# Block inverse of a gated delta step: N used as it stands, forms (U N) transposed at each level

## What is computed

```python
kb = k * beta[..., None]
a_mat = jnp.where(strict, jnp.einsum('bhnid,bhnjd->bhnij', kb, k) * decay, 0.0)
t_mat = lax.linalg.triangular_solve(a_mat + eye, jnp.broadcast_to(eye, a_mat.shape),
                                    left_side=True, lower=True)
u = t_mat @ (v * beta[..., None])
w = t_mat @ (kb * jnp.exp(gc)[..., None])
```

## Time and profile before

| | before |
|---|---|
| median of 3 runs | 2878.22 us |
| profiled execution, first to last instruction | 2873.6 us |
| PE busy | 2854.6 us (99%) |
| DVE busy | 1795.8 us (62%) |
| ACT busy | 1417.1 us (49%) |
| GpSimd busy | 150.7 us (5%) |
| mean DMA rate | 181 GB/s |

### The profile page before, as it was taken

How to read it: one execution, slowest core, us unless ns; L and a number is a source line. 1 busy time by engine, 2 the same in 40 slices (tenths; PEclk the granted TensorE clock), 3 DMA queues, 4 the chain that set the end, 5 groups by cost and what they waited for, 6 DMA issues and landing times.

```text
span 2873.6 us, 68820 instructions
## 1 busy us (share of the span) xinstructions
PE 2854.6 (99%) x25511; PEld 2781.0 (97%) x25511; DVE 1795.8 (62%) x2900; ACT 1417.1 (49%) x2141; POOL 150.7 (5%) x285
## 2 busy tenths in 40 slices
PE   8999999999999999999999999999999999999999
PEld 7999999999999999999999999999999999999999
DVE  7888788888886455555555444587555555554444
ACT  6666566565664444444444343566444444444343
POOL 1112112111110000000000000000000000000000
PEclk9999999999999999999999999999999999999999
DMA  7666656666556555555555555744555555555554
GB/s 226 189 178 188 191 166 194 181 177 188 160 182 198 187 188 178 181 180 178 182 179 180 183 180 181 221 151 130 171 182 179 179 182 178 180 182 179 182 180 152
DMA packets 521091, 518.97 MB, mean 181 GB/s; under 512 B 32128, under 2 KB 444201, under 8 KB 520665
## 3 DMA queue, kind: packets, MB, share of 16 engines
q1 hardware_dynamic: 519150, 510.34, 57.6%
q0 software_dynamic: 1152, 5.58, 0.6%
q10 hardware_dynamic: 594, 0.25, 0.0%
HBM read 492.12 MB, written 32.82 MB: 183 GB/s over the span
## 4 chain that ended last, share of the span: by engine, by line
PE 67%; issue 1%; ACT 0%; DMA 0%; DVE 0%; DVEq 0%; ACTq 0%; POOLq 0%
PE bank L498 11%; PE bank L503 11%; PE bank L499 11%; PE upper L503 11%; PE upper L498 11%; PE upper L499 11%; PE upper L1027 0%; PE upper L1052 0%; DMA x_res<-x_spill 0%; PE upper L1038 0%; PE upper L1089 0%; PE upper L1028 0%; PE upper L1055 0%; ACT scores L812 0%; PE upper L1042 0%
## 5 line engine op out<-in xcount | busy, mean ns | idle before, releaser
L477 DVE TENSOR_TENSOR w_lo<-w_raw,w_hi 128x1024 fp32r<-128x1024 f32 x858 | 1051.2, 1225 | 919.9 <-ACT w_hi L470 917.0
L470 ACT ACTIVATE w_hi<-w_raw 128x1024 fp32r<-128x1024 f32 x858 | 910.1, 1061 | 1241.6 <-PE bank L503 709.1
L498 PE MATMUL bank<-h_hi,w_hi 128*128 128x264 f32 x3168 | 829.6, 295 | 0.4 <-DVE h_lo L585 0.3
L499 PE MATMUL bank<-h_lo,w_hi 128*128 128x264 f32 x3168 | 794.8, 284 | 0.0
L498 PEld LDWEIGHTS bank<-h_hi,w_hi 128*128 128x128 f32 x3168 | 597.3, 189 | 21.3 <-issue 8.8
L499 PEld LDWEIGHTS bank<-h_lo,w_hi 128*128 128x128 f32 x3168 | 598.2, 189 | 1.3
L503 PE MATMUL bank<-h_hi,w_lo 128*128 128x264 f32 x3168 | 449.8, 284 | 0.0
L503 PEld LDWEIGHTS bank<-h_hi,w_lo 128*128 128x128 f32 x3168 | 412.1, 188 | 0.0
L498 PE MATMUL upper<-h_hi,w_hi 128*128 128x264 f32 x1456 | 361.7, 285 | 0.0
L499 PE MATMUL upper<-h_lo,w_hi 128*128 128x264 f32 x1456 | 361.4, 284 | 0.0
L498 PEld LDWEIGHTS upper<-h_hi,w_hi 128*128 128x128 f32 x1456 | 274.3, 188 | 0.0
(11 more groups left out here) (447 smaller groups left out, 3655.5 us busy)
## 6 DMA issues: line engine op xcount, KB each, us to landing
w_raw<-in_w_gate_up_dram SPq DMA_DIRECT2D x704, 256.0 KB, 2.9
w_raw<-in_w_in_a_dram SPq DMA_DIRECT2D x388, 256.0 KB, 3.2
w_raw<-in_w_down_dram SPq DMA_DIRECT2D x352, 256.0 KB, 2.9
w_raw<-in_w_out_a_dram SPq DMA_DIRECT2D x128, 256.0 KB, 3.1
s_dec<-in_state_delta_dram SPq DMA_DIRECT2D x32, 512.0 KB, 6.1
out_dram<-s_dec SPq DMA_DIRECT2D x32, 512.0 KB, 4.9
w_raw<-in_w_q_b_dram SPq DMA_DIRECT2D x64, 256.0 KB, 3.1
w_raw<-in_w_o_b_dram SPq DMA_DIRECT2D x64, 256.0 KB, 2.9
```

The source lines that it names most:

```text
L470: nc.scalar.activation(w_hi[:, s % SPL, :], w_raw[:, s, :], ACT.Copy).then_inc(hi_ready, 1)
L477: ops.tensor_tensor(w_lo[:, s % SPL, :], w_raw[:, s, :], w_hi[:, s % SPL, :].bitcast(F32), ALU.subtract).then_inc(lo_ready, 1)
L498: nc.tensor.matmul(bank[bk][:, 0:T], high(t), xh, start=first, stop=False)
L499: nc.tensor.matmul(bank[bk][:, 0:T], high(t), xl, start=False, stop=False)
```

## The change

The products are formed the other way round. At each level the kernel now computes the transpose of (U N) with `NT` as it stands as stationary operand and the transposed known inverse `Tm` as moving operand. The result `Xm` is then the stationary operand of the second product, and the known inverse, untransposed, the moving one. So no `Nm` is needed: the four TensorE transposes and their copy go. Since in the second product two of the four matrices lie crosswise, ACT makes crosswise copies `Us` of half of `Um` in step 7, and in step 13 a copy of part of `UF` to `Um`. The mask of the 16-wide level is transposed. Because `UF` is the memory of `NT`, and `NT` is now read in step 11, ACT's two copies of the diagonal blocks into `UF` wait for that matmul and stand in step 12. DVE's transpose of the new quarter of `UF` moves from step 13 to step 12, as one instruction, and PE's step 13 waits for it and for ACT's copies. The counts of `inv_pe` fall from 13 to 12 in a group. The diff, cut to this:

```diff
-    halves = [row == col, up & same(16), level(16), level(32)]
+    halves = [row == col, up & same(16), level(16).T, level(32)]
-                Nm = st_("Nm", [P, 4, P])
+                Us = st_("Us", [P, 2, HP])
# ACT
                 elif n == 7:
                     nc.scalar.activation(twos(Um), pair23, ACT.Copy).then_inc(inv_act, 1)
-                    act.wait_ge(inv_pe, 13 * G + 7)
-                    nc.scalar.activation(Nm[:, :, :], B[0][:, :], ACT.Copy).then_inc(inv_act, 1)
-                elif n == 11:
-
-                    act.wait_ge(inv_dve, 15 * G + 10)
+                    for b in range(2):
+                        at, to = slice(HP * b, HP * (b + 1)), slice(HP * (1 - b), HP * (2 - b))
+                        m = nc.scalar.activation(Us[to, :, :], pair23[at, 1, :].rearrange("p (m n) -> p m n", m=2), ACT.Copy)
+                    m.then_inc(inv_act, 1)
+                elif n == 12:
+
+                    act.wait_ge(inv_pe, 12 * G + 9)
                     for b in range(2):
                         at = slice(HP * b, HP * (b + 1))
                         m = nc.scalar.activation(UF[at, :, at], Um[at, :, :], ACT.Copy)
                     m.then_inc(inv_act, 1)
-                elif n == 12:
-                    act.wait_ge(inv_pe, 13 * G + 11)
-                    nc.scalar.activation(Tm[HP:P, 2:4, :], Tm[0:HP, 2:4, :], ACT.Copy).then_inc(inv_act, 1)
                 elif n == 13:
+                    act.wait_ge(inv_dve, 15 * G + 13)
+                    nc.scalar.activation(Um[0:HP, 0:2, :], UF[HP:P, 0:2, HP:P], ACT.Copy).then_inc(inv_act, 1)
# PE
                     each4(pair23, half(Pb), half(Um)).then_inc(inv_pe, 1)
-                    for m_ in range(4):
-                        m = nc.tensor.transpose(B[0][:, m_ * P:(m_ + 1) * P], NT[:, m_, :], ident)
-                    m.then_inc(inv_pe, 1)
                 elif n == 8:
 
+                    inv(inv_dve, 8)
                     inv(inv_act, 6)
-                    each4(pair23, full(Nm), half(Um)).then_inc(inv_pe, 1)
+                    each4(pair23, full(NT), half(Tm)).then_inc(inv_pe, 1)
                 elif n == 10:
                     inv(inv_dve, 9)
-                    each4(pair01, half(Tm), half(Xm)).then_inc(inv_pe, 1)
+                    each4(pair01, half(Xm), lambda m_, b: (Um[block(b), m_, :] if m_ < 2 else Us[block(b), m_ - 2, :])
+                          ).then_inc(inv_pe, 1)
                 elif n == 11:
 
-                    inv(inv_dve, 10)
+                    inv(inv_dve, 11)
...
-                            m = nc.tensor.matmul(B[0][up, m_ * QP:(m_ + 1) * QP], Nm[lo, m_, up],
-                                                 Um[lo, m_, QP:2 * QP], start=True, stop=True)
+                            m = nc.tensor.matmul(B[0][lo, m_ * QP:(m_ + 1) * QP], NT[up, m_, lo],
+                                                 Tm[up, m_, 0:QP], start=True, stop=True)
...
-                            m = nc.tensor.matmul(B[1][up, m_ * QP:(m_ + 1) * QP], Tm[up, m_, 0:QP], Xm[up, m_, 0:QP],
-                                                 start=True, stop=True)
+                            lo, up = quarter(b, 1), quarter(b, 0)
+                            m = nc.tensor.matmul(B[1][up, m_ * QP:(m_ + 1) * QP], Xm[lo, m_, 0:QP],
+                                                 Um[lo, m_, QP:2 * QP], start=True, stop=True)
...
                     inv(inv_act, 7)
-                    inv(inv_dve, 13)
+                    inv(inv_dve, 14)
...
-                            m = nc.tensor.matmul(B[3][block(b), i * HP:(i + 1) * HP], Nm[block(1), m_, block(0)],
-                                                 UF[block(1), m_, block(1)], start=True, stop=True)
+                            m = nc.tensor.matmul(B[3][block(b), i * HP:(i + 1) * HP], NT[block(0), m_, block(1)],
+                                                 Tm[block(0), m_, :], start=True, stop=True)
...
-                            m = nc.tensor.matmul(B[0][block(b), i * HP:(i + 1) * HP], Tm[block(b), 2 * b + i, :],
-                                                 Xm[block(b), i, :], start=True, stop=True)
+                            known = UF[block(1), 2 + i, block(1)] if b else Um[block(0), i, :]
+                            m = nc.tensor.matmul(B[0][block(b), i * HP:(i + 1) * HP], Xm[block(b), i, :], known,
+                                                 start=True, stop=True)
# DVE
                     elif n == 7:
                         dve.wait_ge(inv_act, 9 * G + 5)
-                        nc.vector.transpose(Tm[:, 0:2, :], Um[:, 0:2, :])
-                        for b in range(2):
-                            at, to = slice(HP * b, HP * (b + 1)), slice(HP * (1 - b), HP * (2 - b))
-                            m = nc.vector.transpose(Tm[to, 2:4, :], Um[at, 2:4, :])
-                        m.then_inc(inv_dve, 1)
+                        turned(Tm, Um)
...
                     elif n == 11:
+                        got(9)
+                        nc.vector.tensor_copy(Xm[:, :, 0:QP], m4(B[0][:, 0:P])).then_inc(inv_dve, 1)
+                    elif n == 12:
                         got(10)
-                        nc.vector.tensor_copy(Xm[0:96, :, 0:QP], m4(B[0][0:96, 0:P])).then_inc(inv_dve, 1)
-                    elif n == 12:
-                        got(11)
                         dve.wait_ge(inv_act, 9 * G + 7)
                         for b in range(2):
                             at = HP * b
                             m = ts(UF[at:at + QP, :, at + QP:at + HP], m4(B[1][at:at + QP, 0:P]), -1.0, None, ALU.mult)
                         m.then_inc(inv_dve, 1)
+                        own(13)
+                        nc.vector.transpose(Tm[QP:HP, :, 0:QP], UF[0:QP, :, QP:HP]).then_inc(inv_dve, 1)
                     elif n == 13:
-                        own(13)
-                        dve.wait_ge(inv_act, 9 * G + 8)
-                        for b in range(2):
-                            at = HP * b + QP
-                            m = nc.vector.transpose(Tm[at:at + QP, 2 * b:2 * b + 2, 0:QP],
-                                                    UF[0:QP, 2 * b:2 * b + 2, QP:HP])
-                        m.then_inc(inv_dve, 1)
-                        got(12)
+                        got(11)
                         nc.vector.tensor_copy(Xm[:, 0:2, :], B[3][:, 0:P].rearrange("p (m n) -> p m n", m=2)
                                               ).then_inc(inv_dve, 1)
```

More of the change, by code:

```diff
@@ L1694, in step @@
                 elif n == 4:
-                    act.wait_ge(inv_pe, 13 * G + 1)
+                    act.wait_ge(inv_pe, 12 * G + 1)
                     nc.scalar.activation(twos(Pb), pair01, ACT.Copy).then_inc(inv_act, 1)
                 elif n == 5:
-                    act.wait_ge(inv_pe, 13 * G + 2)
+                    act.wait_ge(inv_pe, 12 * G + 2)
                     nc.scalar.activation(twos(Pa), pair23, ACT.Copy).then_inc(inv_act, 1)
-                    act.wait_ge(inv_pe, 13 * G + 3)
+                    act.wait_ge(inv_pe, 12 * G + 3)
                     nc.scalar.activation(twos(Um), pair01, ACT.Copy).then_inc(inv_act, 1)
                 elif n == 6:
-                    act.wait_ge(inv_pe, 13 * G + 5)
+                    act.wait_ge(inv_pe, 12 * G + 5)
                     nc.scalar.activation(twos(Um), pair01, ACT.Copy).then_inc(inv_act, 1)
                 elif n == 7:
-                    act.wait_ge(inv_pe, 13 * G + 6)
+                    act.wait_ge(inv_pe, 12 * G + 6)
                     nc.scalar.activation(twos(Um), pair23, ACT.Copy).then_inc(inv_act, 1)
-                    act.wait_ge(inv_pe, 13 * G + 7)
-                    nc.scalar.activation(Nm[:, :, :], B[0][:, :], ACT.Copy).then_inc(inv_act, 1)
-                elif n == 11:
-                    act.wait_ge(inv_dve, 15 * G + 10)
+                    for b in range(2):
[4 more added lines that the diff above has]
+                    act.wait_ge(inv_pe, 12 * G + 9)
                     for b in range(2):
@@ L1723, in step @@
                 elif n == 14:
-                    act.wait_ge(inv_pe, 13 * G + 13)
+                    act.wait_ge(inv_pe, 12 * G + 12)
                     for b in range(2):
@@ L1996, in step @@
                         for b in range(2):
-                            up = quarter(b, 0)
-                            m = nc.tensor.matmul(B[1][up, m_ * QP:(m_ + 1) * QP], Tm[up, m_, 0:QP], Xm[up, m_, 0:QP],
-                                                 start=True, stop=True)
+                            lo, up = quarter(b, 1), quarter(b, 0)
+                            m = nc.tensor.matmul(B[1][up, m_ * QP:(m_ + 1) * QP], Xm[lo, m_, 0:QP],
+                                                 Um[lo, m_, QP:2 * QP], start=True, stop=True)
                     m.then_inc(inv_pe, 1)
@@ L2329, in step @@
                 elif 4 <= n <= 13 and n != 9:
-                    got = lambda k: dve.wait_ge(inv_pe, 13 * G + k)
```

(11 more changed lines are left out.)

## The result

The changed kernel takes 2887.97 us, the median of six runs (2887.34 to 2889.12), beside 2877.93 us for the kernel before in the same session (2877.32 to 2879.51). The ratio is 1.0036, with a 95% interval of 1.0026 to 1.0047: 10.0 us slower. Forecast were 8.8 us, 2887.0 us, with a range of 2883 to 2893.

What follows compares the result with a forecast made beforehand. PE was taken as always busy, so only its own instructions and late producers count. Span 2873.6 - 6.2 + 15.0 = 2882.4 us; median 2878.2 + 8.8 = 2887.0 us, 0.3% slower, range 2883 to 2893.

Steps and rivals of the forecast that it cites:

- The transposes: PE, step 7: removing four transposes saves 0.39 us in each of 16 turns, 6.2 us (5.9 to 6.6).
- The wait in step 13: PE waits 0.94 us a turn for ACT's late copies and DVE's transpose, 15.0 us added (13.9 to 18.7).
- the release of PE by DVE: Step 13, last link: PE starts 0.06 us behind the end of DVE's transpose.
- The allowance of 0.1 us for a pipeline that has run dry: Step 13: 0.1 us more allowed above the wait's upper bound of 1.07 us.
- The span: Whole kernel: 2873.6 - 6.2 + 15.0 = 2882.4 us profiled, with the median staying 4.6 us above it.
- Steps 8, 10, 11 and 14: PE: no added cost; about half a microsecond to spare at 8, 11 and 14, small matmuls at 10 unchanged.
- Rival 3: Steps 8, 11, 14: a second wait, spare time overdrawn by 0.3 us, adds 4.8 us, 2891.8 us; chance 0.09.
- Rival 1: Step 13: the wait is hidden and the transposes' saving alone stands, 2872.0 us; chance 0.07.
- Rival 2: Step 7: a transpose costs its 273 ns record, so 17.5 us go, 2875.7 us; chance 0.04.
- Rival 4: After each wait TensorE drops to 1.2 GHz for half a chunk, 23 us, 2910 us; chance 0.01.
- Rival 5: The change doesn't do what it says, the transposes stay in some form, 2893 us; chance 0.01.
- The bounds for the start of the copies: ACT, step 12: copies into `UF` start at 457.14, taken as forecast, or 457.27, the other bound.

Runs made afterwards that it cites:

- seventh experiment: Changed kernel with ACT's copies into `UF` ahead of the split of chunk 7, plus a useless DVE copy in step 12: 2871.72 us, ratio 0.9980.
- third experiment: The first experiment with the four TensorE transposes of step 7 put back, their output unread: 2877.68 us, ratio 1.0001.
- second: Kernel before, with only ACT's two copies into `UF` moved from step 11 to step 12, behind the split of chunk 7: 2889.14 us, ratio 1.0038.
- sixth experiment: Changed kernel with a useless 128x128 DVE copy added in step 12 between scaling and transpose: 2891.74 us, ratio 1.0051.
- first experiment: Changed kernel with ACT's step 12, the two copies into `UF`, moved ahead of its split of chunk 7: 2870.71 us, ratio 0.9977.
- fourth: Changed kernel with only the first of ACT's two copies into `UF` moved back to step 11, the second behind the split: 2883.05 us, ratio 1.0019.
- fifth: Changed kernel with only the second of ACT's two copies into `UF` in step 11, the first behind the split: 2882.39 us, ratio 1.0016.

## Why the prediction was right

**What bounds the kernel.** That only PE's own instructions and late producers count was borne out: ACT and DVE lost work (1.3 and 11.2 us of busy time) and the kernel got slower. The seventh experiment shows it from the other side: work added to DVE costs nothing where there is room.

**The transposes.** 0.39 us a turn were forecast from the starts. In the changed kernel it is 0.62 us from step 7's first small matmul to the second large one (451.96 to 452.58), the value that step 8 had before. The third experiment puts the 6.2 us at 7.0 by its time and at 16 x 0.37 = 5.9 by the length of the turns. (The 16 small matmuls of the prediction are 8: each leaves two records. Nothing hangs on it, since the groups that are compared are alike.) The page of the Trainium skill that was weighed, "TensorE: Matmul & The Clock Gate", section "Part 4: PE-mode transpose", gives some 275 ns for one transpose, and this trace repeats that as the length of a record (273 ns). It is not the cost here: four in a row held the next work up by 0.4 us.

**The wait in step 13.** Forecast was 0.94 us, measured 1.03. Moved by the 5.58 us between the two turns' splits, the forecast chain gives 462.72 for the copies, 463.58 for DVE, 464.51 for the end of the transpose; the trace has 462.73, 463.58 and 464.50. The whole miss lies in the last link. I took 0.06 us for the release of PE by DVE, from the one case in the earlier trace rows. Here 0.15 us pass between the transpose's end and the matmul, in the second and sixth experiments 0.15 and 0.14. Why the release near 70 us was quicker stays open. With it the sum is 16 x 1.03 - 6.2 = +10.3 us, where +10.0 was measured. The allowance of 0.1 us for a pipeline that has run dry was in the range, not in the forecast. The chain through DVE's transpose was right, though the profile names another releaser, ACT's copy to `Um`; the sixth experiment shows that the name was wrong.

**The span.** The forecast span was 2882.4 us; 2885.9 were profiled, 3.5 us more. By the starts the stage lost 16.6 us and gained 16 x 0.35 = 5.6 (0.37 for the transposes, less 0.02 for the new forms), 11 us in all and not 8.8. 1.1 us came ahead of the stage. The 4.6 us between the profiled span and the median, which the prediction said would stay, are 2.1 in the changed kernel. They came of a profiled execution of the kernel before that was faster than its median. So the mechanism was right and the wait was put 1.6 us too low over 16 turns (15.0 against 16.6), and that the median came out within 1.0 us of the forecast owes a little to chance.

**Steps 8, 10, 11 and 14.** No wait in the changed kernel, as forecast. Step 14 follows at 2.03 us, though DVE's `Xm` copy ends only at 466.08, 0.6 us ahead of it. Rival 3 did not come.

**The rivals.** Rival 1, that the wait is hidden, does not hold for the changed kernel. Its saving (6.2 us) is what the first experiment gives (6.4 us) as soon as its condition is met, the copies not behind the split. The kernels of the fourth and fifth experiments lie between. Rival 2 is out by the third experiment. Rival 4 did not show: the granted clock stays at nine tenths or more in all slices. Rival 5 is out by the count of matmul records, 64 fewer.

**The range** of 10 us was wide beside a miss of 1.2 us in the sum. The bounds for the start of the copies (457.14 or 457.27, 0.96 and 1.09 us behind the split) both turned out to be real: 0.97 is what the changed kernel and the fifth experiment show, 1.08 the fourth.

## What to carry to other kernels

Where one engine is busy all the time, removing its work helps by the shift of its next starts, and this is easily lost again by a single dependence that comes late in every turn. When an edit moves an instruction on a helper engine, look at what stands ahead of it in that engine's own program and when that can start: here 0.83 us of copies were moved behind a 1.06 us split that was itself tied to PE, and 17 us hung on that order. Ask first whether a late step can be put ahead of its neighbour, before giving up the form that needs it.

## What was not expected of the hardware

- The ACT copies compared here, each right behind a 128x1024 split, start either 0.97 or 1.08 us behind the split's start. Which of the two it is repeats in all 16 turns of the fourth experiment (1.08) and of the fifth (0.97), but the copy of line 1616, with 128 partitions, has 0.97 in the kernel before and 1.08 in the changed one. The cause is open.
- From the end of the DVE instruction that releases them to the start of the waiting 64x64 matmuls 0.14 to 0.15 us pass, in the changed kernel and in the second and sixth experiments. That is more than twice the 0.06 us read from the one such release in the kernel before.
